# Expert weights of a mixture layer used in place: bf16 heads read from the float32 words, two float32 buffers for each weight

## The reference, cut to what matters

```python
D_MODEL, D_EXPERT, MOE_BLOCK, N_EXPERTS, TOP_K = 1024, 512, 128, 32, 2
...
buf = jnp.zeros((P, D), h.dtype).at[dest].set(ht[tok_s])          # rows of tokens, by expert, blocks of 128
def expert_block(args):
    xblk, e = args
    return (jax.nn.silu(xblk @ w_gate[e]) * (xblk @ w_up[e])) @ w_down[e]
ybuf = lax.map(expert_block, (buf.reshape(nblk, MOE_BLOCK, D), blk_e)).reshape(P, D)
y = (ybuf[dest].astype(F32) * gate_s[:, None]).astype(h.dtype)
out = jnp.zeros((M, D), h.dtype).at[tok_s].add(y)
```

## Time and profile before

| | |
|---|---|
| median of three executions | 1851.29 us (1848.05 to 1852.13) |
| span of the profiled execution, first to last instruction | 1850.6 us |
| the profiled execution against the median | its span lies 0.7 us under it |
| busy over the span: PE, PEld, DVE, ACT, POOL | 1477.0, 934.3, 1159.3, 806.0, 469.0 us |
| 0 to 950 us, mixers | PE 815.4 us busy, granted clock 0.95, 48 GB/s |
| 950 to 1000 us, in the output projection | PE 48.5 of 50 us busy, 53 GB/s |
| 1000 to 1100 us, its end, routing, first gathers | PE 29.8, DVE 51.2, POOL 41.0 of 100 us busy |
| 1135.35 to 1728.55 us, 29 experts | PE 530.1, DVE 464.6, ACT 377.8 of 593.2 us busy, 355 GB/s |
| 1790 to 1851 us, end of the layer | PE 0, DVE 45.5, POOL 38.7 of 61 us busy |
| HBM read, written | 261.33 MB, 39.88 MB |

### The profile page before, as it was taken

The page is one execution under the profiler, slowest core; times in us unless marked ns, Lnnn a source line. Parts: engine busy times, 40 slices in busy tenths (PEclk is TensorE's granted clock), DMA queues, the critical chain, the costliest instruction groups (busy, mean ns, idle before and its releaser), DMA issues.

```text
span 1850.6 us, 21482 instructions
## 1 busy us (share of the span) xinstructions
PE 1477.0 (80%) x8153; PEld 934.3 (50%) x8202; DVE 1159.3 (63%) x1167; ACT 806.0 (44%) x866; POOL 469.0 (25%) x343
## 2 busy tenths in 40 slices
PE   3899899949999999977999229998998899899700
PEld 2565555539999999841454214444444444444300
DVE  6346466655555555424497818778777777877566
ACT  7265533323333333336000316765566566656310
POOL 4400211132222222100654341122112211211075
PEclk9999999969999999986999559999999999989955
DMA  7621111000000000030211458989898898988372
GB/s 207 222 75 42 54 45 35 23 1 1 1 0 0 0 0 0 0 143 1 95 57 46 194 153 335 373 331 372 360 363 343 356 378 353 352 358 361 133 271 95
DMA packets 74639, 302.08 MB, mean 163 GB/s; under 512 B 18128, under 2 KB 40672, under 8 KB 62288
## 3 DMA queue, kind: packets, MB, share of 16 engines
q1 hardware_dynamic: 56976, 239.03, 34.4%
q0 software_dynamic: 17600, 62.20, 8.7%
HBM read 261.33 MB, written 39.88 MB: 163 GB/s over the span
## 4 chain that ended last, share of the span: by engine, by line
PE 45%; DVE 25%; ACT 13%; issue 10%; POOL 4%; DMA 2%; DVEq 0%; POOLq 0%; ACTq 0%; SPq 0%
PE ps L1622 12%; DVE big L1161 7%; PE ps L1591 7%; PE ps L1789 6%; ACT big L1463 6%; PE ps L1815 4%; PE ps L1817 4%; PE ps L1814 4%; PE ps L1628 3%; DVE big L923 3%; PE ps L1611 2%; POOL scr_tok L690 1%; DVE big L1184 1%; DVE big L1176 1%; ACT big L1382 1%
## 5 line engine op out<-in xcount | busy, mean ns | idle before, releaser
L1161 DVE TENSOR_TENSOR big<-big 128x4096 bf16<-128x4096 f32 x96 | 424.1, 4421 | 137.8 <-ACT big L1463 137.8
L1463 ACT ACTIVATE big<-big 128x4096 bf16<-128x4096 f32 x96 | 347.1, 3620 | 224.4 <-PE ps L1817 219.8
L1815 PE MATMUL ps<-big 128*128 128x512 bf16 x768 | 309.0, 402 | 35.9 <-DVE big L1176 31.5
L1814 PE MATMUL ps<-big 128*128 128x512 bf16 x722 | 289.3, 401 | 33.5 <-DVE big L1176 33.5
L1622 PE MATMUL ps<-big 128*128 128x128 f32 x2176 | 272.0, 280 | 17.5 <-DVE big L923 5.7
L1622 PEld LDWEIGHTS ps<-big 128*128 128x128 f32 x2176 | 256.1, 192 | 30.6 <-DVE big L923 9.5
L1591 PE MATMUL ps<-big 128*128 128x347 f16 (+1 forms) x1656 | 255.5, 316 | 16.1 <-DVE big L790 11.3
L1591 PEld LDWEIGHTS ps<-big 128*128 128x128 f16 (+1 forms) x1656 | 163.3, 99 | 111.1 <-issue 16.2
L1817 PE MATMUL ps<-big 128*128 128x512 bf16 x765 | 201.2, 400 | 0.2
L1375 ACT ACTIVATE big<-ps 128x512 f32<-128x512 f32 (+2 forms) x119 | 63.0, 568 | 251.1 <-PE ps L1628 167.8
L1814 PEld LDWEIGHTS ps<-big 128*128 128x128 bf16 x768 | 77.8, 101 | 171.5 <-DVE big L1176 76.5
(11 more groups left out here) (270 smaller groups left out, 1673.0 us busy)
## 6 DMA issues: line engine op xcount, KB each, us to landing
big<-in_w_exp_gate_dram SPq DMA_DIRECT2D x32, 2048.0 KB, 10.2
big<-in_w_exp_up_dram SPq DMA_DIRECT2D x32, 2048.0 KB, 9.2
big<-in_w_exp_down_dram SPq DMA_DIRECT2D x32, 2048.0 KB
scr_y<-big POOLq DMA_DIRECT2D x32, 512.0 KB, 8.3
big<-in_w_in_dram SPq DMA_DIRECT2D x22, 512.0 KB, 3.7
scr_h<-big POOLq DMA_DIRECT2D x16, 512.0 KB, 4.1
scr_y<-big POOLq DMA_DIRECT2D x1, 8192.0 KB, 26.1
big<-scr_h SPq DMA_DIRECT2D x16, 512.0 KB, 4.1
```

The lines of the kernel that those rows point to most:

```text
L1161: v.tensor_tensor(wsp[s][k][1], raw[k], wsp[s][k][0], ALU.subtract).then_inc(s_lo[k], 1)
L1463: f(wsp[s][k][0], raw[k], ACT.Copy).then_inc(s_hi[k], 1)
L1814: mm(out_, x[0][:, k, :], w[0][:, k, cs], start=k == 0, stop=False)
L1815: mm(out_, x[0][:, k, :], w[1][:, k, cs], start=False, stop=False)
```

## The change

The upper 16 bits of a float32 are themselves a bf16, the number cut off after 8 bits. The head of a weight is no longer written by ScalarE: `upper` gives a view of the float32 buffer in which each element is the upper half of a word, one bf16 every 4 bytes. TensorE takes this view as the moving operand for both products with w_head, and VectorE subtracts it from the float32 to get the rest, as bf16, packed, into `low[s][k]`.

The buffers change with it. `raw` has two float32 buffers for each weight, and the bf16 heads are gone. SP loads expert n into `raw[n % 2]`. For the first two experts it waits only until what lay there before is no longer used. After that it waits for TensorE: weight k of expert n waits for product k of expert n-2. VectorE's `rest` waits for the load itself. ScalarE copies the whole output of 1024 columns, and VectorE's `yout` is gone.

```diff
-        raw = [RM.take(KD, FE), RM.take(KD, FE), RM.take(KF, D)]
-        wsp = [[halves(RM, KD, FE), halves(RM, KD, FE), halves(RM, KF, D)] for _ in range(2)]
+        raw = [[RM.take(KD, FE), RM.take(KD, FE), RM.take(KF, D)] for _ in range(2)]
...
+        low = [[RM.take(KD * FE // 2).bitcast(BF16).rearrange("p (k c) -> p k c", c=c) for c in (FE, FE, D)] for _ in range(2)]
...
+        def upper(w):
+
+            p, kk, n = w.shape
+            return w.bitcast(BF16).rearrange("p k (c two) -> p k c two", two=2)[:, :, :, 1]
...
-            def weights(n, e):
+            def weights(s, n, e):
                 srcs = (("w_exp_gate", KD), ("w_exp_up", KD), ("w_exp_down", KF))
                 for k, (name, kk) in enumerate(srcs):
-                    if first(n):
-
-                        sp.wait_ge(*((F_O.sem, F_O.at(NT - 1, "o1")) if k < 2 else (F_D.sem, F_D.at(NT - 1, "xhat"))))
+                    if isinstance(n, int) and n < 2:
+
+                        if n == 0 and k == 0:
+                            sp.wait_ge(F_O.sem, F_O.at(NT - 1, "o1"))
+                            sp.wait_ge(F_D.sem, F_D.at(NT - 1, "xhat"))
+                        if n == 1 and k == 0:
+                            sp.wait_ge(F_E.sem, F_E.at(NT - 1, "lg"))
+                            for b in range(2):
+                                sp.wait_ge(s_h1st[b], 16 * 4)
                     else:
 
-                        sp.wait_ge(s_hi[k], n)
-                        sp.wait_ge(s_lo[k], n)
-                    sp.dma_start(raw[k], a[name][0, bass.ds(e, 1)].rearrange("o (p k) n -> p (o k) n", k=kk)).then_inc(s_we[k], 16)
-
-            weights(0, 0)
-            with sp.Fori(1, NE) as i:
-                weights(i, i)
+                        sp.wait_ge((E_G, E_U, E_Y)[k], n - 1)
+                    sp.dma_start(raw[s][k], a[name][0, bass.ds(e, 1)].rearrange("o (p k) n -> p (o k) n", k=kk)).then_inc(s_we[s][k], 16)
+
+            weights(0, 0, 0)
+            weights(1, 1, 1)
+            with sp.Fori(1, NE // 2) as i:
+                weights(0, i * 2, i * 2)
+                weights(1, i * 2 + 1, i * 2 + 1)
...
             def store(s, n):
 
-                pl.wait_ge(V_Y, n + 1)
                 pl.wait_ge(A_Y, n + 1)
...
             def rest(s, n, k):
 
-                dv.wait_ge(s_hi[k], n + 1)
-                v.tensor_tensor(wsp[s][k][1], raw[k], wsp[s][k][0], ALU.subtract).then_inc(s_lo[k], 1)
+                dv.wait_ge(s_we[s][k], (n - s) * 8 + 16)
+                if not (isinstance(n, int) and n < 2):
+                    dv.wait_ge((E_G, E_U, E_Y)[k], n - 1)
+                v.tensor_tensor(low[s][k], raw[s][k], upper(raw[s][k]), ALU.subtract).then_inc(s_lo[k], 1)
...
-            def head(s, n, k):
-
-                ac.wait_ge(s_we[k], n * 16 + 16)
-                if not (isinstance(n, int) and n < 2):
-
-                    ac.wait_ge((E_G, E_U, E_Y)[k], n - 1)
-                f(wsp[s][k][0], raw[k], ACT.Copy).then_inc(s_hi[k], 1)
-
...
-                f(yb[s][:, 0:512], ps[:, 5, :], ACT.Copy).then_inc(A_Y, 1)
+                f(yb[s], ps[:, 5:7, :].rearrange("p b c -> p (b c)"), ACT.Copy).then_inc(A_Y, 1)
...
             def split_product(out_, x, w, kk, cs):
 
+                w = (upper(w[0]), w[1])
+
                 for k in range(kk):
                     mm(out_, x[0][:, k, :], w[0][:, k, cs], start=k == 0, stop=False)
...
-                    last = split_product(ps[:, 5 + hf, :], hTe[s], wsp[s][2], KF, slice(hf * 512, (hf + 1) * 512))
+                    last = split_product(ps[:, 5 + hf, :], hTe[s], (raw[s][2], low[s][2]), KF, slice(hf * 512, (hf + 1) * 512))
```

More of the change, by code:

```diff
@@ L347, in build @@
         RM = Region(BASE)
-        raw = [RM.take(KD, FE), RM.take(KD, FE), RM.take(KF, D)]
-        wsp = [[halves(RM, KD, FE), halves(RM, KD, FE), halves(RM, KF, D)] for _ in range(2)]
+        raw = [[RM.take(KD, FE), RM.take(KD, FE), RM.take(KF, D)] for _ in range(2)]
         xg = [RM.take(D) for _ in range(2)]
+        hs = [RM.take(FE) for _ in range(2)]
+        RM = Region(AFTER)
+        low = [[RM.take(KD * FE // 2).bitcast(BF16).rearrange("p (k c) -> p k c", c=c) for c in (FE, FE, D)] for _ in range(2)]
         xT = [halves(RM, KD, P) for _ in range(2)]
-        hs = [RM.take(FE) for _ in range(2)]
         hd = [RM.take(FE) for _ in range(2)]
@@ L357, in build @@
         assert RM.at <= KEEP, RM.at
-        s_we = [sem(f"s_we{k}") for k in range(3)]
-        s_hi = [sem(f"s_hi{k}") for k in range(3)]
+        def upper(w):
+            p, kk, n = w.shape
+            return w.bitcast(BF16).rearrange("p k (c two) -> p k c two", two=2)[:, :, :, 1]
+        s_we = [[sem(f"s_we{i}{k}") for k in range(3)] for i in range(2)]
         s_lo = [sem(f"s_lo{k}") for k in range(3)]
@@ L364, in build @@
         A_X, A_S, A_H, A_Y = (sem(f"s_a{n}") for n in "xshy")
-        V_X, V_M, V_H, V_Y = (sem(f"s_v{n}") for n in "xmhy")
+        V_X, V_M, V_H = (sem(f"s_v{n}") for n in "xmh")
         s_yo = [sem(f"s_yo{i}") for i in range(2)]
@@ L492, in _ @@
                     e = sp.value_load(oei[0:1, j:j + 1], min_val=0, max_val=NE - 1)
-                    weights(NE + j, e)
+                    weights(j % 2, NE + j, e)
             for s in range(2):
@@ L1196, in turn @@
                     rest(1 - s, n + 1, 2)
-                if not first(n):
-                    yout(1 - s, n - 1)
             for k in range(3):
@@ L1210, in _ @@
             hidden(1, NE - 1)
-            yout(1, NE - 1)
             n_over = dv.value_load(novi[0:1, 0:1], min_val=0, max_val=OVER)
@@ L1220, in _ @@
                     hidden(s, n)
-                    yout(s, n)
             for ti in range(NT):
@@ L1481, in yout @@
                     ac.wait_ge(s_yo[s], (n - s) * 8)
-                f(yb[s][:, 0:512], ps[:, 5, :], ACT.Copy).then_inc(A_Y, 1)
+                f(yb[s], ps[:, 5:7, :].rearrange("p b c -> p (b c)"), ACT.Copy).then_inc(A_Y, 1)
             def turn(s, n, more=True):
-                if more:
-                    head(1 - s, n + 1, 0)
                 silu(s, n)
@@ L1491, in turn @@
                     rows_in(1 - s, n + 1)
-                    head(1 - s, n + 1, 1)
-                    head(1 - s, n + 1, 2)
                 if not first(n):
                     yout(1 - s, n - 1)
[L1498 to L1502, removed]
             rows_in(0, 0)
@@ L1517, in _ @@
                     rows_in(s, n)
-                    for k in range(3):
-                        head(s, n, k)
                     silu(s, n)
@@ L1824, in gate @@
                     pe.wait_ge(A_S, n)
-                split_product(ps[:, 2, :], xT[s], wsp[s][0], KD, slice(0, FE)).then_inc(E_G, 1)
+                split_product(ps[:, 2, :], xT[s], (raw[s][0], low[s][0]), KD, slice(0, FE)).then_inc(E_G, 1)
             def up(s, n):
@@ L1830, in up @@
                     pe.wait_ge(V_M, n)
-                split_product(ps[:, 3, :], xT[s], wsp[s][1], KD, slice(0, FE)).then_inc(E_U, 1)
+                split_product(ps[:, 3, :], xT[s], (raw[s][1], low[s][1]), KD, slice(0, FE)).then_inc(E_U, 1)
             def turned(s, n):
```

5 lines of the change are left out of this document (removed).

## The result

Four executions of the changed kernel took 2050.29 to 2053.08 us, median **2051.39 us**. The kernel before took 1849.67 us beside it (four executions). The ratio is 1.1099, 95% interval 1.1069 to 1.1129: 11% slower. Forecast were 2066 us and a range of 2000 to 2172.

A forecast was written before the change was run, and what follows sets the result against it. No engine was full; a loop of waits set 20.46 us an expert. New period 27.8 us: 1850.6 + 213.0 (loop) - 3.9 + 5.2 (ends) + 0.4 (last copy) = 2065.3 us, forecast 2066, range 2000 to 2172.

The forecast's parts named there:

- The loop and its place: Expert stage: down product end, down load, gate load, subtraction, hidden rows, next down product; 27.8 us a period against 20.46.
- The loads: Down product's end to gate subtraction's start: 0.3 us to issue, 15.3 for two loads, 0.1 to start; 15.7 us.
- The rest of the loop: From the gate subtraction's start through hidden rows and down product to its end: 12.1 us, unchanged.
- price: Low clock after a wait: a down product's 24 matmuls would take 5.2 us, take 7.0; same price taken as before.
- the pause at 1101.76: Earlier trace: after some 3 us without work, slow matmuls ended within 3.3 us; used to keep the clock term unchanged.
- The sum: Whole span: 1850.6 + 213.0 - 3.9 + 5.2 + 0.4 = 2065.3 us; forecast 2066 us.
- The ends: Outside the loop: down(0) ends at 1131.5, -3.9 us; after the loop 28.5 us, +5.2, wider last copy 0.4.
- The stride: TensorE's moving operand at a 4-byte step in 48 of 72 matmuls, and VectorE's subtraction reading strided: both taken as nothing.
- The half rate: Rival: TensorE's strided reads at half rate, 0.21 us more a strided matmul, loop 31.2 us, 2172 us; 9%.
- What the profile would show: Signs: three loads within 1 us after each down product, gate landing about 15 us later, TensorE near 66% busy, DMA near 0.66.
- hidden loads: Rival: loads always there when VectorE asks, DMA engines bound at 18.7 us an expert, 1796 us; 5%.
- Loads sharing the engines: Rival: the three loads share the DMA engines, gate lands with up 5.3 us later, 2220 us; 2%.

The follow-up runs named there:

- the expectation above: Changed kernel with TensorE reading the packed rest instead of the strided upper half; 16 matmuls, 0.2 us an expert, 2040 to 2050 us expected; measured 2055.81 us.
- the run with both orders: Changed kernel with SP loading gate and up of n+2 ahead of down of n+1, and VectorE's down subtraction one turn later: 1760.6 us, ratio 0.9514.
- SP's order alone: Changed kernel with only SP's loads reordered, gate and up of expert n+2 ahead of down of n+1: 2018.67 us, ratio 1.0888.
- both orders and packed reads: Changed kernel with SP's loads reordered, VectorE's down subtraction one turn later, and TensorE reading the packed rest, not the strided upper half: 1745.07 us, ratio 0.9435.
- the hidden rows first: Changed kernel with one exchange on VectorE, hidden rows of n-1 ahead of the gate subtraction of n+1, SP's order kept: 1816.91 us, ratio 0.9804.
- the run of the releaser: Kernel before, with SP's load of a weight of expert n also waiting for TensorE's product of expert n-2: 2100.44 us, ratio 1.1357.
- the reordered kernel before: Kernel before, with SP loading gate and up of n+1 ahead of down of n, and down conversion and subtraction one turn later: 1805.67 us, ratio 0.9768.

## Why the prediction was right

*The loop and its place*: right, step by step. SP issues down, gate and up right behind a down product, VectorE is late with the gate subtraction, TensorE with the down product.

*The loads*: 15.7 us were forecast from the end of the product to the start of the gate subtraction, and it is 14.2 to 14.4 (1402.97 to 1417.17, or 1417.33 by the chain). SP's issue follows the product in 0.02 us, where 0.3 was taken. The gate load lands 14.2 us after the down issue, where the earlier trace rows had 15.3 and the earlier trace rows 12.9. The choice was the nearer in kind, the truth lay between. How the engines shared their time between the loads and the 1.05 MB of store and gather I have not measured apart. The prediction's 5.3 us a load is 5.5 by its own rows (12.9 - 7.4), and here down and gate land 6 us apart; no term of the sum went by it.

*The rest of the loop*: 12.1 us were forecast, and it is 12.95 (1417.33 to 1430.28). The term that was too small is the clock: the down product takes 8.0 us instead of 7.0. TensorE in windows of a microsecond (PE busy first, the clock third from the end):

```profile
1416.00:1417.00 1.00, 0.00 (x0) 0.00 (x0) 0.00 (x0) 0.00 (x0) 0.00 (x0) 1.00 0.98 410
1417.00:1418.00 1.00, 0.00 (x0) 0.00 (x0) 0.83 (x1) 0.00 (x0) 0.00 (x0) 0.63 0.84 356
1418.00:1419.00 1.00, 0.00 (x0) 0.00 (x0) 1.00 (x1) 0.00 (x0) 0.00 (x0) 0.50 1.27 541
1426.00:1427.00 1.00, 1.00 (x4) 0.36 (x3) 1.00 (x1) 0.00 (x0) 0.00 (x0) 0.50 0.00 0
1428.00:1429.00 1.00, 1.00 (x7) 0.40 (x5) 0.26 (x1) 0.00 (x0) 0.00 (x0) 1.00 0.00 0
```

TensorE had stopped at 1415.1. It was granted 2.4 GHz to 1417 and 1.2 GHz from within the microsecond after, and took up work at 1422.3. At the low clock are the first 12 of the 24 matmuls (0.43 us apart to 1427.55 in the chain). Forecast were about 8: 1.8 us of price at 0.21 us each. I had taken the pause at 1101.76 as the measure, which was 3 us, where this is 7.

*The sum*: two errors, some -1.4 and +0.85 us, partly cancel, and that they did is luck: 27.26 against 27.8, 29 x 0.54 = 16 us, nearly the whole difference of 2066 to 2051.

*The ends*: down(0) ends at 1131.06 (forecast 1131.5). From down(29) to the last copy's start it is 28.9 us (28.5).

*The stride*: taken as nothing, it is 0.01 us a matmul where the clock is full. In the loop that is the 8 strided matmuls in the second half of a down product, 0.1 us, some 2 us in all. (The 16 matmuls and 0.2 us of the expectation above are too many: at the low clock strided and packed matmuls are both 0.43 us apart.) VectorE's subtraction, taken as unchanged, takes 4422 ns with the strided operand, 4421 before. The Trainium skill's rule (Advanced Engine Details and Errata, "SBUF Cachelines") has full speed for a step of 4 bytes. The trace shows 5% less, and the measurement decides. The half rate is refuted.

*What the profile would show*: TensorE's busy share was forecast at 66% and is 73%. Four more matmuls a product at the low clock (0.85 us) and 48 strided ones (0.5 us) make most of the difference of 1.7 us an expert. The other signs came as forecast.

*The rivals*: hidden loads give 1761 us, as the run with both orders shows, where 1796 was worked out (with 392 GB/s; it is 420 to 427). What the rival lacked was not buffers but two changes of order. The Trainium skill's advice to double-buffer (Trainium Kernel Development and Optimization, "Best Practices") pays here with both orders (1761 us), not with the change's own (2051 us) and not with SP's order alone (2019 us), where the loads are issued in the order in which their buffers come free. Loads sharing the engines is refuted: the changed kernel's profile page has 8.1, 13.5 and 18.8 us to landing for down, gate and up, one after the other.

## What to carry to other kernels

When a conversion is removed by using the loaded buffer in place, its lifetime grows from "until converted" to "until multiplied", and the load behind it moves from the fast engine's release to the slowest one's. After such a change look at who releases each load, what is queued behind it on the issuing queue, and what each in-order engine does ahead of the instruction that the bound engine waits for. Here the same edit is 11% slower or 5% faster than before, by the order of the loads and of one subtraction alone. Most of the way, 234 of 291 us, is the swap of two instructions on VectorE.

## What had not been expected of the hardware

- A bf16 moving operand at a step of 4 bytes costs 5% at full clock (0.228 against 0.218 us for 128 x 512). At the low clock both are 0.43 us apart in these traces.
- The DMA engines moved 426 GB/s over 400 us in the kernel with both orders and packed reads, where the kernel before moved 355 over its stage.
- POOL's gather takes 4.03 us as a median in the kernel before and 0.99 in the changed one, with the same shape. In the first it runs while VectorE subtracts (1410.66, VectorE busy 1409.41 to 1413.83), in the second while VectorE waits for a load (1405.26); with both orders it is 3.75 us again. The traces say more than the medians. In the stretches around 1400 us, where a gather starts well within a subtraction, it ends 0.85 to 0.87 us after that subtraction: 1414.70 after 1413.83 in the kernel before, 1408.36 after 1407.50 with the hidden rows first, 1416.84 after 1415.98 in the run of the releaser, 1422.48 after 1421.63 with both orders and packed reads, where it takes only 1.60 us. So the subtraction holds the gather up. Where the gather starts within 0.03 us of the subtraction's start (both at 1397.7 in the reordered kernel before) it takes 0.98 us, and POOL's plain store issue takes 0.56 us beside a subtraction (1409.80, kernel before) and without one. No run changed this by itself, and the gather was on no chain shown here.
